# One half of a weight chunk, and one split of weights, moved in the seam between the second cross attention and the second block's last feed-forward

## The reference

```
c = memory_cross_attention_2(h, mem_n, xa_wq[l], xa_wkv[l], xa_wo[l])   # ends with o @ xa_wo
x = x + rmsnorm_2(c, xa_post_g[l])

h = rmsnorm_2(x, ffn2_pre_g[l])
f = swiglu(h, ffn2_w_gate[l], ffn2_w_up[l], ffn2_w_down[l])             # silu(h @ w_gate) * (h @ w_up)
x = x + MACARON_WEIGHT * rmsnorm_2(f, ffn2_post_g[l])
```

## Time and profile before

| | |
|---|---|
| median of 3 runs | 1172.95 us (1172.7 to 1174.29) |
| the profiled execution, its own time | 1173.07 us |
| its span (first to last instruction) | 1171.4 us |
| granted TensorE clock, mean over the span | 0.998 |
| TensorE matmul busy | 1145.2 us (98%) |
| VectorE busy | 812.5 us (69%) |
| ScalarE busy | 622.3 us (53%) |
| chain that ended last, by engine | PE 83%, DVE 10%, ACT 4%, issue 2% |

### The profile page before, as it was taken

How to read it: one execution, slowest core, us unless ns; L and a number is a source line. 1 busy time by engine, 2 the same in 40 slices (tenths; PEclk the granted TensorE clock), 3 DMA queues, 4 the chain that set the end, 5 groups by cost and what they waited for, 6 DMA issues and landing times.

```text
span 1171.4 us, 16802 instructions
## 1 busy us (share of the span) xinstructions
PE 1145.2 (98%) x6765; PEld 999.7 (85%) x6765; DVE 812.5 (69%) x881; ACT 622.3 (53%) x801; POOL 82.1 (7%) x114
## 2 busy tenths in 40 slices
PE   8999999999999999999999999999999998999997
PEld 7978898889987799999888888888777887888886
DVE  6897658756878568787548777547776747777743
ACT  7666446436478466565345444436456547444432
POOL 7101100200000000000000000002700000000000
PEclk9999999999999999999999999999999999999999
DMA  8654333334665354655655655555633534665560
GB/s 259 190 158 147 99 106 110 109 108 156 220 198 181 108 163 156 204 169 191 216 179 181 210 179 186 200 195 177 201 116 127 180 108 127 194 202 182 179 214 36
DMA packets 144420, 193.95 MB, mean 166 GB/s; under 512 B 6168, under 2 KB 121240, under 8 KB 144344
## 3 DMA queue, kind: packets, MB, share of 16 engines
q1 hardware_dynamic: 143144, 188.43, 49.7%
q0 software_dynamic: 1200, 4.46, 1.1%
HBM read 191.82 MB, written 1.05 MB: 165 GB/s over the span
## 4 chain that ended last, share of the span: by engine, by line
PE 83%; DVE 10%; ACT 4%; issue 2%; DMA 0%; DVEq 0%; ACTq 0%
PE banks L1328 23%; PE banks L1362 19%; PE banks L1310 13%; PE banks L1331 11%; DVE wlo L1920 4%; PE banks L1347 3%; PE banks L1338 2%; PE banks L1589 1%; PE banks L1477 1%; ACT whi L1649 1%; PE banks L1464 1%; PE banks L1376 1%; PE banks L1547 1%; DMA x_tok<-in_x 0%; DVE x_tok L2193 0%
## 5 line engine op out<-in xcount | busy, mean ns | idle before, releaser
L1920 DVE TENSOR_TENSOR wlo<-raw,whi 128x2048 fp32r<-128x2048 f32 (+1 forms) x178 | 406.5, 2291 | 122.5 <-ACT whi L1649 122.4
L1649 ACT ACTIVATE whi<-raw 128x2048 fp32r<-128x2048 f32 (+1 forms) x179 | 340.1, 1903 | 248.3 <-PE banks L1331 146.0
L1328 PE MATMUL banks<-xhl,whi 128*128 128x512 f32 x1232 | 396.2, 403 | 2.7 <-DVE y5l L2248 1.8
L1331 PEld LDWEIGHTS banks<-xhl,wlo 128*128 128x128 f32 x1232 | 231.4, 188 | 54.6
L1331 PE MATMUL banks<-xhl,wlo 128*128 128x256 f32 x1232 | 242.6, 278 | 0.0
L1328 PEld LDWEIGHTS banks<-xhl,whi 128*128 128x128 f32 x1232 | 188.9, 189 | 10.3 <-issue 5.6
L1310 PE MATMUL banks<-xhl,whi 128*128 128x256 f32 x912 | 165.5, 284 | 1.3 <-DVE xhl L1947 0.7
L1310 PEld LDWEIGHTS banks<-xhl,whi 128*128 128x128 f32 x912 | 142.0, 192 | 2.1 <-DVE xhl L1947 1.1
L1310 PE MATMUL banks<-xhl,wlo 128*128 128x256 f32 x456 | 129.0, 283 | 0.0
L1362 PE MATMUL banks<-whi,hh 128*128 128x512 f32 x264 | 102.9, 390 | 0.0
L1362 PE MATMUL banks<-wlo,hh 128*128 128x512 f32 x264 | 102.7, 389 | 0.0
(11 more groups left out here) (368 smaller groups left out, 1531.9 us busy)
## 6 DMA issues: line engine op xcount, KB each, us to landing
raw<-in_w_in SPq DMA_DIRECT2D x40, 1024.0 KB, 5.3
raw<-in_w_up SPq DMA_DIRECT2D x22, 1024.0 KB, 5.8
raw<-in_ffn_w_gate SPq DMA_DIRECT2D x22, 1024.0 KB, 5.3
raw<-in_ffn_w_up SPq DMA_DIRECT2D x22, 1024.0 KB, 5.3
raw<-in_ffn_w_down SPq DMA_DIRECT2D x22, 1024.0 KB, 5.0
raw<-in_w_down SPq DMA_DIRECT2D x11, 1024.0 KB, 5.6
raw<-in_w_out SPq DMA_DIRECT2D x8, 1024.0 KB, 5.2
raw<-in_xa_wkv SPq DMA_DIRECT2D x8, 1024.0 KB, 5.7
```

Source lines behind the costliest of these rows:

```text
L1328: pe.matmul(bank(b[m]), wh[:, k, m * P:(m + 1) * P], both[:, k, :, :].rearrange("p a t -> p (a t)"), start=(k == 0), stop=(k == KD - 1), s ...
L1331: ins = pe.matmul(bank(b[m])[:, 0:T], wl[:, k, m * P:(m + 1) * P], Xh[:, k, :], start=False, stop=(k == KD - 1), skip_group_check=True)
L1649: act.activation(columns(whi, c, part), columns(raw, c, part), ACT.Copy).then_inc(act_done, 1)
L1920: dve.tensor_tensor(columns(wlo, c, part), columns(raw, c, part), columns(whi, c, part), ALU.subtract).then_inc(dve_done, 1)
```

## The change

Three edits. R1 also becomes `by_token`. The seam begins one chunk earlier (with R1 in place of R2): it runs part 0 of R1, R2 and R3 one after the other, and part 1 of R1 and R2 after them. G0's split is taken out of the start of the seam and put behind token half 0's norm, and the second half of R3's part 1 (six matmuls) stands behind the first eight transposes.

```diff
@@ build_chunks @@
     rows("xa_wo_2", 4, "y5", "post", 0)
-    for ch in out[-2:]:
+    for ch in out[-3:]:
         ch["by_token"] = True
@@ seam @@
-        last_, gate_ = c + 1, c + 2
-        pl.ready[c], pl.ready[last_] = ready["y5", chunks[c]["j"]], ready["y5", chunks[last_]["j"]]
+        last_, gate_ = c + 2, c + 3
+        for k in (c, c + 1, last_):
+            pl.ready[k] = ready["y5", chunks[k]["j"]]
...
-        split(c + LEAD)
+        split(last_)
+        while any(step not in pl.number for step in pl.ready[c]):
+            hook(True)
         pl.add("pe", "mm", c, 0)
+        drain()
+        pl.add("pe", "mm", c + 1, 0)
         part_of(0, 0)
         post_half(last_, 0, 0)
         part_of(0, 1)
...
         root(name, 0)
+        pl.add("pe", "mm", c + 1, 1)
+        split(gate_)
         part_of(1, 0)
         post_half(last_, 1, 0)
-        part_of(1, 1)
         for j in groups:
             pl.take(("nt", name, j), (base + j % 4,), ("nl2", name, 1, turns(name)[j][-1]))
         pl.bank_wait["nt", name, 4] = [("nl2", name, 0, turns(name)[0][-1])]
         for j in groups:
             pl.add("pe", "nt2", name, 0, j)
+        part_of(1, 1)
         halves_of(0, 0)
         post_half(last_, 1, 1)
@@ build_plan @@
     mm(c)
-    mm(c + 1)
-    drain()
-    seam(c + 2, "ffn2_pre_g_2", 4)
+    seam(c + 1, "ffn2_pre_g_2", 4)
```

## The result

The changed kernel took 1177.16 us (median of 9 runs, 1175.66 to 1179.75), the kernel before in the same comparison 1174.29 us (9 runs, 1172.7 to 1175.91). The ratio is 1.003, 95% interval 1.002 to 1.0041: slower, by 2.3 to 4.8 us. The profiled execution took 1177.16 us with a span of 1175.4.

What follows compares the result with a forecast made beforehand. TensorE, full outside the seam, was taken as the bound, the seam's path running through the end of token half 1's rows. The three edits summed to +2.8 us on the median: 1172.95 + 2.8 = 1175.8, range 1174.6 to 1177.5.

Steps and rivals of the forecast that it cites:

- R1 by token: Seam's start: twelve matmuls moved behind let R3's part 0 and token half 0's chain start 2.72 us earlier.
- G0's split inside the seam: VectorE and ScalarE: the split's 2.29 and 1.92 us eat the 2.72 won; `nl2(0, 0)` ends up +0.09.
- The load of U1: Queue behind G0's `lo`: issued 7.2 us later, at 973.7, landing about 979, still hidden.
- R3's last matmuls behind the transposes: TensorE in the seam: six matmuls wait behind the eighth transpose, delaying G0's second block; the deciding term, +2.8 us.
- three signs of being wrong: Seam: `nl2(0, 0)` much before 974.4, R3's last six done by 973, or G0's second block before 978.
- half clock reaches R3's last matmuls: Seam: R3's last six run at 1.2 GHz, 1.36 us more; +4.2, 1177.1; chance 0.2.
- The case at +2.2: Seam: the clock does not fall, or falls less, and 0.6 us come off; 1175.2; chance 0.1.
- the eighth transpose would not hold what stands behind it: TensorE in the seam: R3's end stays as early, or the split ends earlier; +0.1, 1173.05; chance 0.1.
- The faster case: Seam: token half 0's norm alone is the path, gate up to 1.6 us earlier; 1171.35, or 1170.2; chance 0.04.

Runs made afterwards that it cites:

- e1: The changed kernel with R3's six last matmuls ahead of all eight transposes again; ratio 0.9995 to the kernel before.
- e3: The changed kernel with only the eighth transpose behind R3's six last matmuls, the first seven staying ahead; ratio 1.0004 to the kernel before.
- e8: The kernel before with only G0's split moved behind token half 0's norm; ratio 1.0022 to the kernel before.
- e2: The kernel before with only R3's six last matmuls moved behind the eight transposes; ratio 1.0028 to the kernel before.
- e5: The kernel before with `nh2` and `nl2` of token half 0's blocks 1 and 2 ahead of token half 1's second `post1` and `post0`; ratio 1.0004.
- e4: The changed kernel run again without alteration, beside as many runs of the kernel before; ratio 1.0023.
- e6: The changed kernel with `lo` of G0 moved on VectorE to behind `nl2(0, 0)`; ratio 1.0013 to the kernel before.

## Why the prediction was right, and where it was wrong

Set on the clock of the profile before (1.43 us off each time after):

| step | predicted | measured |
|---|---|---|
| R3's part 0 starts | 961.97 | 961.98 |
| root of token half 0 done | 969.37 | 969.38 |
| `lo` of G0 starts | 971.35 | 971.22 |
| `post0` of token half 1 | 973.68 | 973.55 |
| `nl2(0, 0)` | 974.48 | 974.34 |
| the eighth transpose | 974.97 | 974.83 |
| R3's six last matmuls | 975.20 | 974.89 |
| `post1`, second column half | 976.80 | 976.61 |
| `post0`, second column half | 977.56 | 977.39 |
| G0's second block | 980.15 | 979.97 |

**R1 by token**: right, R3's part 0 began 2.71 us earlier, and in e1 and e3, where the split spends that, nothing was gained. **G0's split inside the seam**: right that it eats the head start, and e8 shows it. `hi` began 0.11 earlier than said (970.72 - 1.43 = 969.29 against 969.40), and `lo` and `post0` with it came 0.13 earlier. The load of U1 was issued at the shifted time and stayed hidden: from 992 us to 1160 TensorE's only wait is the 0.6 us for `lo` of U0 that was there before. **R3's last matmuls behind the transposes**: right in mechanism and place (e2, e3), said 2.8, measured 2.62. None of the three signs of being wrong came. The six began 0.31 before the predicted time, 0.17 of it because they stand 0.06 and not 0.23 behind the eighth transpose and 0.14 through `lo`'s earlier start; they took 1.47 instead of 1.36, and so 0.18 is left at G0's second block.

**The rivals.** That half clock reaches R3's last matmuls did not happen: they follow each other by 0.23 us. The prediction put the pause ahead of them at 1.1 us more than before; it was 1.8 more (2.40 against 0.61 on the eighth transpose's row), and the clock still held. The fall came after the second pause, as in the forecast. The seam of the changed kernel has waits of 5.7 us in place of 2.5 and the same 3.4 us at 1.2 GHz; e1 waits 2.6 us and e8 5.4, and both have 6.8. The page "TensorE: Matmul & The Clock Gate" of the Trainium skill (Part 1) says that the default is throttled and that activity releases it. That more pause would then mean more time at 1.2 GHz, as the prediction read it, these profiles don't bear out. The case at +2.2, a seam without half clock, has none of the nine profiles to try it on. What the prediction had no case for is a stretch twice as long in the seam: without reaching R3's matmuls it added 0.65 to 1.35 us in e1, e2 and e8. That the eighth transpose would not hold what stands behind it is refuted by the row at 976.32. The same page of the Trainium skill (Part 2) says that matmuls stay in program order, and e3 against the change agrees: the six came 2.7 us earlier when only the eighth transpose's place, ahead of them or behind, was changed. The faster case never had its condition: `nl2(0, 1)` was later, not earlier.

The measured 1177.16 us lies in the range (1174.6 to 1177.5), near its upper end. **The step that failed** is the one that set the sum on a time: "I set the sum on the median: 1172.95 + 2.8 = 1175.8". I took the three runs shown for one value with small scatter. They were two of the fastest kind (about 1172.9) and one slower. Over nine runs the kernel before has a median of 1174.29, and 1175.8 lies only 1.5 above that, while the medians are 2.9 apart and the ratio stands for 3.5. The measured 1177.16 is 1.41 above 1172.95 + 2.8: 1.34 of it is the base (1174.29 for 1172.95), -0.16 the seam's term (2.64 for 2.8), and 0.23 is not placed and within the scatter. That the time still fell in the range owes something to luck, since the range was set on the same base and was wide for another reason, the clock in the seam. What the prediction put at nothing, without a reason, is half clock outside the seam: the profiles show none, one or (e2) two such stretches in parts that the change doesn't touch, at 1.1 to 1.6 us each. That the first nine runs gave 1.003, and the next nine 1.0023, is within the intervals of both.

## What to carry to other kernels

In an engine that runs in order, work that is ready must not be put behind an instruction that waits for another engine, if that engine in turn waits for the work: here one transpose of 128x128, waiting for a bank, held six matmuls and through them two engines for 2.6 us. To make one chain of a seam earlier gains nothing while the seam's end hangs on another chain; find which wait ends last first. In e3 the first seven transposes began 1.6 us earlier after `y5l` than before (972.81 - 957.41 = 15.40, against 973.09 - 956.10 = 16.99), and in e5 G0's second block came 1.75 earlier, and U0 gained nothing in either (31.94 and 33.04 for 31.99). And before a forecast is set on a time, look at whether the runs lie in steps: the difference of the traces, taken from an unchanged instruction just ahead of the change, told 2.62 us where medians of nine runs said 2.9 and the ratio 3.5.

## What the runs showed of the hardware that was not expected

- The whole program's time moves with stretches of some 3.4 us at 1.2 GHz, at places that are the same in several kernels but not in each of their runs. Near 400 us four profiles had one (the change, e2, e3, e8) and five had none (before, e1, e4, e5, e6); near 845 us two had one (e2, e6) and seven had none, with the same instructions at both places. What decides it, no run here shows. In e2:

```profile
845.00:850.00 5.00, 5.00 (x18) 3.45 (x17) 4.08 (x8) 1.48 (x5) 0.00 (x0) 0.66 0.67 222
```

  A stretch does not cost the same everywhere: 1.6 us near 400, 1.1 near 845, 0.65 to 1.35 for a second one in the seam. `y5l` starts at 955.79 to 956.10 in the four profiles with no stretch ahead of it, at 957.02 with the one near 845, at 957.39 to 957.53 with the one near 400 and at 958.61 with both (958.61 - 957.53 = 1.08, the price of the one near 845). The parts add up to the time of a run: e2's profiled execution had them all, 1172.91 (the kernel before with its one stretch) + 2.68 (seam) + 1.6 + 1.1 + 1.24 = 1179.5, and took 1179.54 us.
- In the seam the stretch is 3.4 us in some profiles and twice that in others. In e1 it was 6.8, and in e3, whose seam differs in one transpose, 3.4:

```profile
975.00:980.00 5.00, 3.41 (x18) 3.27 (x18) 4.01 (x12) 4.22 (x14) 0.64 (x2) 0.70 0.83 292
980.00:985.00 5.00, 4.90 (x28) 4.69 (x27) 1.43 (x5) 2.88 (x6) 0.00 (x0) 0.62 0.02 7
```

```profile
975.00:980.00 5.00, 2.40 (x15) 2.07 (x15) 4.43 (x11) 4.12 (x13) 0.64 (x2) 0.93 0.70 210
980.00:985.00 5.00, 4.66 (x30) 4.45 (x30) 2.29 (x7) 4.13 (x10) 0.00 (x0) 0.73 0.31 105
```

  The first fence is e1, the second e3. The doubled stretch made U0 1.35 us later in e1, 1.24 in e2 and 0.65 in e8, counted from G0's second block, and in none of them did it move that block itself.
- A matmul whose inputs are long ready starts 0.06 us after the start of the transpose that waited (976.26 and 976.32); G0's first matmul of token half 0, which needed the same `nl2`, had started 0.23 after it. That need is not the reason by itself: behind the eighth transpose of token half 1 G0's first matmul needs the same `nl2` too, and it starts 0.06 after it (983.49 and 983.55 before). What makes the distance stays open.
